# GpSimd takes the halves' copies from ScalarE, and DMA turns the probabilities and merged tiles in a hybrid attention layer

## What is computed

```python
aq, ak, av, az, bqkv, bz, bbeta, balpha, gate_a, gate_b = jnp.split(h @ w_in, cuts, axis=-1)
ya = moba_attention(to_heads(aq), to_heads(ak), to_heads(av)) * jax.nn.silu(az)
bqkv = short_conv(bqkv, conv_w)
...
o = gated_delta_rule(to_bhsd(bq), to_bhsd(bk), to_bhsd(bv), ...)
o = rms_norm(o.transpose(0, 2, 1, 3), dn_norm_gain).astype(x.dtype) * jax.nn.silu(to_heads(bz))
merged = (jax.nn.sigmoid(gate_a) * (ya @ w_branch_a)
          + jax.nn.sigmoid(gate_b) * (yb @ w_branch_b))
return x + merged @ w_out
```

## Time and profile before

| | |
|---|---|
| median of 3 runs | 789.0 us (788.03 to 789.43) |
| the profiled execution | 788.17 us, span 786.4 us |
| busy, share of the span | PE 97%, PEld 80%, DVE 70%, ACT 59%, POOL 13% |
| TensorE's granted clock | full speed in all 40 slices of the page |
| DMA | 152.89 MB, mean 194 GB/s |

### The profile page before, as it was taken

One profiled execution on the slowest core, in us unless ns is written; L12 is line 12 of the kernel. 1 busy time (PEld: TensorE's weight loads), 2 busy tenths in 40 slices (PEclk: granted clock), 3 DMA queues, 4 the chain that ended last, 5 costly groups with the idle time before them and its releaser, 6 DMA issues.

```text
span 786.4 us, 10433 instructions
## 1 busy us (share of the span) xinstructions
PE 764.7 (97%) x3507; PEld 627.6 (80%) x3507; DVE 553.3 (70%) x1265; ACT 467.6 (59%) x697; POOL 102.1 (13%) x167
## 2 busy tenths in 40 slices
PE   8998999999999999999999999999999999999996
PEld 6887887888788878878887788788778888888884
DVE  5779748965895698479658956884797566765563
ACT  5686557656764766477567556764765764435440
POOL 5112010110101020101101010111020100001120
PEclk9999999999999999999999999999999999999999
DMA  9968757876687778668766877687676576688652
GB/s 250 247 169 199 201 161 188 220 193 173 184 221 198 177 194 209 174 177 219 193 172 179 214 207 172 180 206 201 172 193 199 176 197 189 181 264 272 192 160 108
DMA packets 219333, 152.89 MB, mean 194 GB/s; under 512 B 49168, under 2 KB 184336, under 8 KB 219152
## 3 DMA queue, kind: packets, MB, share of 16 engines
q1 hardware_dynamic: 219136, 151.96, 71.6%
q10 hardware_dynamic: 144, 0.26, 0.1%
HBM read 140.64 MB, written 2.11 MB: 182 GB/s over the span
## 4 chain that ended last, share of the span: by engine, by line
PE 67%; DMA 9%; ACT 8%; DVE 7%; SPq 5%; issue 4%; DVEq 0%; POOLq 0%; POOL 0%; ACTq 0%
PE pj L602 20%; PE pj L600 20%; PE pj L601 20%; DMA turned<-halves 9%; SPq L334 3%; DVE w_lo L1146 3%; ACT w_hi L865 2%; ACT moT L916 1%; ACT convs L935 1%; SPq L298 1%; ACT L947 1%; DVE kk L1299 1%; ACT yT L916 1%; PE pj L851 1%; PE pj L849 1%
## 5 line engine op out<-in xcount | busy, mean ns | idle before, releaser
L1146 DVE TENSOR_TENSOR w_lo<-w_raw,w_hi 128x1024 fp32r<-128x1024 f32 x251 | 307.5, 1230 | 157.3 <-ACT w_hi L865 155.9
L600 PE MATMUL pj<-w_hi,xt_hi 128*128 128x512 f32 x860 | 345.9, 402 | 0.4 <-DVE w_lo L1146 0.4
L602 PE MATMUL pj<-w_hi,xt_lo 128*128 128x512 f32 x860 | 336.6, 391 | 0.0
L601 PE MATMUL pj<-w_lo,xt_hi 128*128 128x512 f32 x860 | 335.9, 391 | 0.0
L865 ACT ACTIVATE w_hi<-w_raw 128x1024 fp32r<-128x1024 f32 x251 | 263.5, 1054 | 118.4 <-PE pj L602 106.6
L602 PEld LDWEIGHTS pj<-w_hi,xt_lo 128*128 128x128 f32 x860 | 161.4, 188 | 34.3
L600 PEld LDWEIGHTS pj<-w_hi,xt_hi 128*128 128x128 f32 x860 | 161.8, 188 | 32.2 <-issue 0.6
L601 PEld LDWEIGHTS pj<-w_lo,xt_hi 128*128 128x128 f32 x860 | 161.9, 188 | 31.1
L1333 DVE SCALAR_TENSOR_TENSOR xs<-lrep,xs 128x31 f32<-128x31 f32 (+30 forms) x496 | 80.0, 231 | 0.0
L535 POOL TENSOR_TENSOR xo<-v,own 128x128 f32<-128x128 f32 x16 | 14.7, 919 | 125.3 <-DVE v L1342 87.3
L1273 DVE SCALAR_TENSOR_TENSOR conv<-kk,hs,conv 128x255 f32<-128x255 f32 (+2 forms) x72 | 29.7, 475 | 0.0
(11 more groups left out here) (292 smaller groups left out, 734.6 us busy)
## 6 DMA issues: line engine op xcount, KB each, us to landing
w_raw<-in_w_in_dram SPq DMA_DIRECT2D x384, 256.0 KB, 3.4
w_raw<-in_w_out_dram SPq DMA_DIRECT2D x64, 256.0 KB, 3.7
w_raw<-in_w_branch_a_dram SPq DMA_DIRECT2D x32, 256.0 KB, 3.6
w_raw<-in_w_branch_b_dram SPq DMA_DIRECT2D x32, 256.0 KB, 3.7
gate<-in_x_dram SPq DMA_DIRECT2D x8, 256.0 KB, 5.3
gate<-in_x_dram SPq DMA_DIRECT2D x4, 512.0 KB, 7.1
gate<-in_final_norm_gain_dram SPq DMA_DIRECT2D x1, 1024.0 KB, 9.4
out_dram<-gate SPq DMA_DIRECT2D x4, 256.0 KB, 3.5
```

Of the source, the lines that this page charges most:

```text
L600: pe.matmul(bank[:, t, :], hi[:, k, tok], w_hi[:, slot, cs], start=(k == 0), stop=False)
L601: pe.matmul(bank[:, t, :], hi[:, k, tok], w_lo[:, slot, cs], start=False, stop=False)
L602: mm = pe.matmul(bank[:, t, :], lo[:, k, tok], w_hi[:, slot, cs], start=False, stop=(k == kt_all - 1))
L1146: dve.tensor_tensor(w_lo[:, slot, :], w_raw[:, slot, :], w_hi[:, slot, :].bitcast(F32), ALU.subtract).then_inc(lo_ready, 1)
```

## The change

GpSimd takes all copies apart and joins that ScalarE did. The probabilities are taken apart on GpSimd, turned by a transfer behind unit 2 of the next head (`J_P`), and joined. The merged tiles go the same way in the branch B stage (`M_TURNED`), a chunk later than before. The slots are moved: the Gram products from 28 to 26, `SUB` and all that follows two slots earlier, q k^T (`M_QK`) from 38 to 40, probabilities times v (`M_PV`) from 44 to 50. In the branch A stage the units of the first two chunks are interleaved (`A_ORDER`). The SiLU of the gates has slots of its own (`S_Z`, `M_Z`).

```diff
+M_TURNED = [FIRST_B + BU * (c + 1) + 7 for c in range(NC)]
+A_ORDER = [(0, 0), (0, 1), (0, 2), (1, 0), (1, 1), (1, 2), (0, 3), (1, 3)] + [(c, j) for c in (2, 3) for j in range(4)]
+A_LAST = [max(n for n, (at, _) in enumerate(A_ORDER) if at == c) for c in range(NC)]
...
-S_NAT, S_HALVES, S_DEC, S_JOIN, S_TURN, S_CONV, S_SILU, S_KK, S_BACK = 15, 17, 18, 21, 22, 24, 26, 28, 42
+S_NAT, S_DEC, S_TURN, S_Z, S_CONV, S_SILU, S_KK, S_BACK = 15, 18, 20, 20, 22, 24, 26, 38
...
-J_YA, J_DN, J_YB, J_MO, J_BACK = 5, 14, 16, 22, 23
-SUB = {33: (0, 2), 34: (2, 4), 35: (4, 7), 36: (7, 9), 37: (9, 12), 38: (12, 14), 39: (14, 17), 40: (17, 19), 41: (19, 22),
-       42: (22, 23), 43: (23, 26), 44: (26, 28), 45: (28, 31)}
-S_V = 45
-S_Y, S_XY, S_XT = [48, 54], [50, 56], 52
-S_Y0, S_R1, S_Y1, S_O, S_YB, S_YT = 59, 61, 63, 65, 68, 72
+J_P, J_YA, J_DN, J_YB, J_BACK, J_MO = 2, 6, 14, 15, 20, 21
+SUB = {31: (0, 2), 32: (2, 4), 33: (4, 7), 34: (7, 9), 35: (9, 12), 36: (12, 14), 37: (14, 17), 38: (17, 19), 39: (19, 22),
+       40: (22, 23), 41: (23, 26), 42: (26, 28), 43: (28, 31)}
+S_V = 43
+S_Y, S_XY, S_XT = [46, 52], [48, 54], 50
+S_Y0, S_R1, S_Y1, S_O, S_YB, S_YT = 57, 59, 61, 63, 66, 74
...
-M_NAT, M_HALVES, M_JOIN, M_QK, M_EXP, M_PT, M_PV, M_YA, M_YT = 31, 33, 37, 38, 40, 42, 44, 46, 51
+M_NAT, M_Z, M_QK, M_EXP, M_PV, M_YT = 31, 36, 40, 42, 50, 56
...
+            def turn_p(h):
+                sp.wait_ge(p_halves_ready, h + 1)
+                sp.dma_start_transpose(turned[:, 0:6, :], p_halves).then_inc(p_landed, 16)
             def turned_behind(h, j):
+                if h and j == J_P:
+                    turn_p(h - 1)
                 if h and j == J_YA:
                     sp.wait_ge(ya_halves, h)
                     turn_y(ya_landed)
...
+                    number = c * units + (first_unit + j)
+                    load(wmat, col, j, number)
+                    if number in M_TURNED:
+                        at = M_TURNED.index(number)
+                        sp.wait_ge(m_apart, T * at + T)
+                        sp.dma_start_transpose(m_halvesT, m_halves).then_inc(m_landed, 16)
...
+            for n, (c, j) in enumerate(A_ORDER):
+                load(w_a, c * CH, j, FIRST_A + n)
+                if n == J_P:
+                    turn_p(H - 1)
+                if n == J_YA:
+                    sp.wait_ge(ya_halves, H)
+                    turn_y(ya_landed)
...
+            def joined(m, mT, ready):
+                pool.tensor_copy(apart(m), mT).then_inc(ready, 1)
...
+                if not first:
+                    pool.wait_ge(q_squared, T * h)
+                for t in range(T):
+                    pool.wait_ge(dn_nat_ready, T * h + t + 1)
+                    pool.tensor_copy(dn_halves[:, :, :, t, :],
+                                     dn_nat[:, t, 0:3 * P].bitcast(U16).rearrange("p (a n e) -> p a e n", a=3, e=2)
+                                     ).then_inc(dn_halves_ready, 1)
                 if not first:
                     output_norm(h - 1)
+                    yb_apart(h - 1)
+                    pool.wait_ge(o_done, h)
+                pool.wait_ge(dn_landed, 16 * h + 16)
+                for a in range(3):
+                    joined(u[:, a, :], dn_halvesT[:, 4 * a:4 * a + 4, :].rearrange("p (e t) n -> p e (t n)", e=2), u_ready)
...
+                if not first:
+                    yb_joined(h - 1)
...
+                for t in range(T):
+                    pool.wait_ge(mo_nat_ready, T * h + t + 1)
+                    pool.tensor_copy(halves[:, :, :].rearrange("p e (a t n) -> p e a t n", a=2, t=T)[:, :, :, t, :],
+                                     mo_nat[:, t, 0:2 * P].bitcast(U16).rearrange("p (a n e) -> p e a n", a=2, e=2)
+                                     ).then_inc(mo_halves_ready, 1)
...
+                joined(dn_nat[:, 0, :], back_halvesT.rearrange("p (e b) n -> p e (b n)", e=2), back_ready)
+                pool.wait_ge(mo_landed, 16 * h + 16)
+                joined(moT[:, :, :].rearrange("p a n -> p (a n)"), turned[:, :, :].rearrange("p (e b) n -> p e (b n)", e=2),
+                       moT_ready)
+                pool.wait_ge(prob_ready, T * h + T)
+                pool.tensor_copy(p_halves.rearrange("p (e n) -> p e n", e=2), apart(prob[:, :])).then_inc(p_halves_ready, 1)
+                pool.wait_ge(v_ready, (LEVELS + 1) * h + 1)
+                pool.tensor_tensor(xo[:, :], v[:, :], own[:, 0, :], ALU.mult).then_inc(xo_ready, 1)
+                if not first:
+                    pool.wait_ge(pv_done, h)
+                pool.wait_ge(p_landed, 16 * h + 16)
+                joined(probT[:, :], turned[:, 0:6, :].rearrange("p (e b) n -> p e (b n)", e=2), pt_ready)
+                pool.wait_ge(ya_ready, T * h + T)
+                pool.tensor_copy(halves[:, 0, :].rearrange("p (e n) -> p e n", e=2),
+                                 apart(ya[:, :, :].rearrange("p t n -> p (t n)"))).then_inc(ya_halves, 1)
+                pool.wait_ge(v_ready, (LEVELS + 1) * h + 2)
+                pool.tensor_tensor(xo[:, :], v[:, :], own[:, 1, :], ALU.mult).then_inc(xo_ready, 1)
+                if not first:
+                    pool.wait_ge(yb_lo_ready, h)
+                pool.wait_ge(ya_landed, 16 * h + 16)
+                joined_y(yaT_ready)
...
+            yb_apart(H - 1)
+            yb_joined(H - 1)
...
+            for c in range(NC):
+                for t in range(T):
+                    pool.wait_ge(merged, T * c + t + 1)
+                    pool.tensor_copy(m_halves.rearrange("p (e i t n) -> p e i t n", e=2, i=4, t=T)[:, :, :, t, :],
+                                     gate[:, NC + c, t, :].bitcast(U16).rearrange("p (i n e) -> p e i n", i=4, e=2)
+                                     ).then_inc(m_apart, 1)
+                if c > 0:
+                    pool.wait_ge(mT_lo_ready, 2 * c)
+                pool.wait_ge(m_landed, 16 * c + 16)
+                for i in range(2):
+                    joined(mT[:, i * CH:(i + 1) * CH],
+                           m_halvesT.rearrange("p (e b) n -> p e b n", e=2)[:, :, 4 * i:4 * i + 4, :].rearrange(
+                               "p e b n -> p e (b n)"), mT_done)
...
                     pe.matmul(E[:, P:3 * P], moT[:, 0, P:2 * P], moT[:, 1, :], start=True, stop=True).then_inc(qk_done, 1)
-                if s == M_PT:
-                    pe.wait_ge(prob_ready, T * h + T)
-                    for i in range(3):
-                        mm = pe.transpose(C[:, i * P:(i + 1) * P], prob[:, i * P:(i + 1) * P], ident[:, :])
...
-            def turn_merged(c):
-                pe.wait_ge(merged, T * c + T)
-                ps = [dn_ps, mo_ps][c % 2]
...
-                for half in range(2):
-                    for q in range(4):
-                        i, t = 2 * half + q // 2, q % 2
-                        mm = pe.transpose(ps[:, (4 * half + q) * P:(4 * half + q + 1) * P],
-                                          gate[:, NC + c, t, i * P:(i + 1) * P], ident[:, :])
-                    mm.then_inc(mT_done, 1)
+            for n, (c, j) in enumerate(A_ORDER):
+                def free(t, c=c):
+                    if c == 0:
+                        pe.wait_ge(gate_ready, T * (H - 1) + t + 1)
+                    elif c == 1:
+                        pe.wait_ge(mo_nat_ready, T * H)
+                    else:
+                        pe.wait_ge(a_gated, T * (c - 2) + t + 1)
+                def between(t, n=n):
+                    dn_step(T * n + t + SLOTS, H - 1)
+                    mo_step(T * n + t + SLOTS, H - 1)
+                if n == A_ORDER.index((0, BU - 1)):
+                    pe.wait_ge(ya_lo_ready, H)
+                unit(n % RING, FIRST_A + n, ya_hi, ya_lo, UK * j, pj[c % 2], H, free, between)
...
+            for n in range(NC * BU):
+                dn_step(2 * n + SLOTS, H - 1)
+                mo_step(2 * n + SLOTS, H - 1)
+                tail_split(FIRST_A + n + LEAD)
+                dn_step(2 * n + 1 + SLOTS, H - 1)
+                mo_step(2 * n + 1 + SLOTS, H - 1)
+                if n - 2 in A_LAST:
+                    gate_a(A_LAST.index(n - 2))
```

209 lines of the change are left out of this document (70 added, 139 removed).

## The result

The changed kernel takes 845.96 us in the median (844.55 to 846.61), the kernel before 788.51 us beside it: 1.0726 times as long, 95% interval 1.0706 to 1.0745. The sign of the forecast was right, the size was not: 807 us was forecast, with a range to 820, and the loss is 57 us, not 18.

A forecast was written before the change was run, and what follows sets the result against it. The prediction took TensorE, busy 97% of the span, as the bound. It summed 788.2 − 2.7 − 3.6 − 7.3 + 22 + 5 + 5 = 806.6 for the profiled execution, forecasting 807 us, range 775 to 820.

The forecast's parts named there:

- What bounds the kernel: Whole kernel: TensorE, busy 97%, sets the time; in the heads VectorE runs full beside it, 0.87 us apart.
- what TensorE loses: Transpositions −2.7 and −3.6 us, waits for moT −7.3 us; TensorE alone would reach 774.6 from 788.2.
- What GpSimd does to VectorE: Gram products to xe: GpSimd's copies hold two-input VectorE operations 2.9 us a head, a sixth taken off; bounds 0 and 3.5.
- meet nothing: GpSimd's two copies of the old order last the same in every head to 1%, so nothing makes them wait.
- copies of 16 bits do not hold VectorE: Rival, Gram products to xe: the +22 falls away and part of a +5; 775 to 786 us, chance 0.24.
- TensorE then waits 2.7 us a head: +22 us: At the product behind xe, 8 heads: VectorE's 2.9 us delay less 0.2 us of cushion.
- Ahead of K: Before the Gram products' start (K): TensorE's wait grows 0.6 us a head, +5 us in all, from −3 to +10.
- `gate_a`: Branch A stage: draining chunk 0 makes TensorE's unit 8 wait once, +5 us, from 0 to 7.
- The output stage: Behind the heads: weight transfers start 4 to 5 us later, with some 3 us of room; taken as 0, bound +4.
- in part: Rival, Gram products to xe: GpSimd slips into VectorE's waits, delay about 1.6 us a head; 789 to 798 us, chance 0.16.
- SyncE becomes the brake: Rival, in the heads: weight transfers held back, TensorE waits for w_lo once or twice a head; 818 to 835 us, chance 0.14.
- The time passes 789 at c = 0.75 us: With c the delay in a head: time about 774.6 + 10 + 8 × (c − 0.2), both fives in.

The follow-up runs named there:

- Run 8: Run 7 with probabilities times v two slots later, at 52: 775.7 us, 0.9861 of the kernel before.
- run 3: The changed kernel with four attention copies (two apart, moT's join, the probabilities' copy apart) back on ScalarE, slots kept: 816.4 us (1.0375).
- run 5: Run 4 with the way-back join on ScalarE too, and the two edits of run 2: 799.3 us (1.0162).
- run 7: Run 6 with the way-back join on ScalarE instead of GpSimd: 782.0 us (0.9935).
- run 9: The changed kernel, all copies on GpSimd, with the delta rule's old slots, probabilities times v at 52, and run 2's edits: 814.0 us (1.0347).
- run 11: The kernel before, with five extra GpSimd products a head behind the way-back join, which nobody waits for: 792.0 us (1.0063).
- Run 1: The changed kernel with 26 unused transpositions put ahead of TensorE's wait for xe in each head: 836.2 us (1.0626).
- run 4: The changed kernel with all of the heads' copies on ScalarE except the way back's, slots kept: 817.3 us.
- run 6: Run 4's copies and run 2's edits, with the delta rule's slots of the kernel before; attention keeps its new slots: 788.2 us (1.001).
- run 2: The changed kernel with gate_a of chunk 0 one unit earlier and the final gain's transfer behind the second w_out chunk: 836.6 us (1.0631).

## Why the prediction was wrong

**What bounds the kernel, what TensorE loses.** Right. The wait for `moT` is gone, as are the transpositions. Run 8 keeps these gains and avoids most of the costs. That its 775.7 us is so near the 774.6 taken for TensorE alone is in part luck: it won 10.9 us over the kernel before beside it, not 13.6, with 3.3 us of wait for the Gram products gone and other short waits in their place.

**What GpSimd does to VectorE.** Right in mechanism (runs 3, 5, 7, 9, 11), right in place and nearly in size: 3.4 us a head against 2.9 taken and a bound of 3.5; from K to `xe` 32.85 us against 29.3 + 2.9, and for TensorE's own work 29.56 against 29.6. The sixth taken off for work that is not held did not exist in this layout. The wait came to 26.5 us against 22. That the two old copies "meet nothing" was a wrong reading: their own lengths do not vary, but the way-back join held `mx`. The rival that copies of 16 bits do not hold VectorE (chance 0.24) could have been priced lower from that row.

**The step that failed: "TensorE then waits 2.7 us a head: +22 us".** The sum priced a wait at its own length and put the clock behind it at nothing. Behind 3.3 us without work TensorE ran its next products at the low clock, in seven of eight heads: 1.7 us each, 11.9 us. With the first head's wait for `w_lo` and the two waits behind the heads it is 20.4 us. Run 1 shows the part at `xe` alone. The kernel before has waits of at most 2.1 us and full clock on the whole page, so its trace could not show the price; it could have warned that waits of over 3 us are outside what it shows, and no upper bound was taken for that.

**"Ahead of K", mis-sized.** Forecast +5 with a bound of +10, measured 13.0 − 3.3 = +9.7. The contention that I named is not the cause: with all copies on ScalarE the wait is the same, 1.77 us (run 4). The slots are, as in the old ones it is gone (run 6). K came 2.7 us sooner, and I had the chain gain back more of it than it did. The traces point at one link. From its first step to its last the convolution takes 7.4 us in the changed kernel and in runs 3, 4 and 5 (6.9 or 7.0 in the first head), 6.0 to 6.3 in the kernel before, and 5.8 in runs 6 and 7 (6.2 in the first head). The gate's SiLU stands in the slot of `S_TURN` in the slow ones; in run 4 a `w_hi` starts only behind it, a `w_lo` waits 1.14 us for that, and the last convolution steps stand behind the `w_lo`. But run 9 has the SiLU there and the 7.4 us too, and only one of its eight heads waits. So the link is too long only for the earlier slots; moving the SiLU alone was not tested.

**Behind the heads.** `gate_a`: forecast 5, measured 4.6, and run 2 shows it as order. The output stage, costed at 0 with a bound of +4: a wait of 4.29 us, over the bound. The room of 3 us was read from rows of before with SyncE's queue as it was there; its final-gain transfer now waits for a join on GpSimd, and the weights wait behind it. That is part of the wait; 2.64 us stay without it (run 2). In the first head another wait of 3.1 us for `w_lo` was not foreseen: that `w_lo` stands behind convolution steps, for which VectorE sat idle 3.26 us until GpSimd's joins came. With the joins on ScalarE (run 4) no wait for `w_lo` in a head is over 0.9 us.

**The forecast's sum against the trace.** To the 806.6 forecast for the profiled execution add 20.4 for the clock, 4.5 more at `xe`, 4.7 more at the Gram products, 4.3 in the output stage and 3.5 for `w_lo` in the heads, less 0.4 at `gate`: 843.6 of the 844.55 us measured. The clock is the largest term, and 807 would have been missed by half as much with it in.

**The parts against the whole**, each from two runs, by their ratios: the edits behind the heads 7.5 us (run 2); the old slots, with probabilities times v at 52, 22.3 (run 2 to run 9); the copies back to ScalarE 38.2 (run 9 to run 8). That is 68 us, and less the 10.9 that run 8 wins over before it is the loss of 57. The order in which one undoes them shifts the parts, since a wait that is long enough to bring the low clock costs more in company.

**The rivals.** That the copies do not hold, or in part: refuted. That SyncE becomes the brake: no wait of a head names it, only the output stage's. "The time passes 789 at c = 0.75 us" rested on the right picture with the wrong price beyond it.
